# Weight rounding at the joints of side-by-side blocks, a gelu moved one block on, a root with more steps around it

## The chip, the cores and the metric

The kernel runs on one core of one Trainium2 chip. The metric is device time in microseconds (us) of one execution, the median of the runs shown. The engines are TensorE (PE, with its weight loads as PEld), VectorE (DVE), ScalarE (ACT), GpSimd (POOL), and SyncE (SP), which issues most DMAs. Each works through a queue of its own and waits for the others by semaphores.

## The reference, cut to what matters

Three transformer-like blocks on 512 tokens of 1024 channels. All of it is fp32. The change touches how the weights of six linears reach TensorE, and the two pieces of elementwise work below.

```python
# first block, mixer: retention, normed by head, gated, then the output linear
yr = _retention_chunkwise(qh, kh, v, log_gamma)
mu = jnp.mean(yr, axis=-1, keepdims=True)
var = jnp.mean(jnp.square(yr - mu), axis=-1, keepdims=True)
yr = (yr - mu) * lax.rsqrt(var + EPS)
y_ret = jax.nn.silu(g) * (yr * gn_w + gn_b)
y_mix = jnp.concatenate([y_ssd, y_ret], axis=-1) @ w_out
...
# third block, mixer: spatial gating, matrix memory and sparse attention, gated and summed
z = h @ w_in
def gmlp_mixer(u_pre, v_pre, ln_g, ln_b, ws, bs):
    u = jax.nn.gelu(u_pre)
    v = layer_norm(jax.nn.gelu(v_pre), ln_g, ln_b)
...
merged = sigmoid(ga) * y_a + sigmoid(gb) * y_b + sigmoid(gc) * y_c
```

## The kernel before

A linear reads its weights from HBM in slabs through a ring of two slots (`weight_ring`). Each tile of 128 output channels takes one unit of weights (128x1024; in `w3_up_a` 128x512). To keep fp32 precision with fast matmuls, ACT rounds a unit to its high half (`weights_hi`), POOL subtracts to get the low half (`weights_lo`), and PE makes three products of each of eight k steps: high by high, high by low activations, low by high. There are two buffers for units (UNITS = 2), so ACT rounds unit n+2 when PE is done with tile n. Activations are split in the same way, the high half on ACT (L780, L992) and the low half on DVE (L804, L1049).

`linears_beside` runs linears beside other work. It is called five times, one Block each, and every Block ends with a barrier of all engines:

| Block | linears, tiles | work beside | next linear |
|---|---|---|---|
| state space | w_z, 8 | state-space heads | w_g |
| retention | w_g, 8 | retention | w_mixu |
| mix | w_mixu, 8 | head norms of retention | w_mixr |
| sparse attention | mqk, mo, gu, gv, 24 | attention | w3_ga |
| gated memory | ga, gb, gc, 24 | spatial gating, matrix memory | w3_up_a |

The other work is written as generators, one for PE and one for ACT, which are cut into quanta by `yield`. A slot is one k step of three matmuls. `due` says how many quanta must have run by a slot: `min(quanta, 1 + int(slot * (quanta - 1) / (share * slots)))`. PE runs the quanta that are due behind a slot. ACT has no slots of its own: for tile n it runs all quanta that are due by the tile's last slot, then rounds unit n+2 (`high`, L770, which waits until PE is done with tile n), then takes the tile out of its bank (`take`, L1446 or the like). DVE runs its side work in one row.

`split_ahead` gives the rounding of the next linear's first units, `s.ahead` says to the next Block how many are there. Before the change it is called for both units, and ACT does this after everything else of the Block:

```python
            if beside.act_end:
                beside.act_end(act)
            act.wait_ge(s.units_done.sem, unit0 + count)
            next_high(act)
```

`act_end` is used once: sparse attention gives `gelu`, which applies gelu to `s.gv` (L3797).

In `mix` a head's mean and variance are matmuls (L1940, L1945), the squares are on ACT (L1974), the root is on ACT (L1977) and its reciprocal on DVE (L1997). `spreads` (L1952) puts it on all partitions, and DVE applies it (L2001, L2002). In gated memory the spatial gating is mean (L3134), centring (L3141), squares (L3146), variance (L3151), root (L3156), scaling (L3163), shift (L3169) and transposes (L3181). A head of the matrix memory is scores (L3261), weighing (L3300, L3303) and values (L3270), and `finish` (L3310 to L3312) frees the banks of the head before.

Of the kernel before, what the change touches and what calls it, by code (L numbers as in the profile page):

```python
# [18 lines left out]
ACT = mybir.ActivationFunctionType  # L19
# [3 lines left out]
P = 128  # L23
# [298 lines left out]
UNITS = 2  # L322
UNIT_K = 8
# [354 lines left out]
def linears_beside(s, parts, beside):  # L678

    ahead, s.ahead = s.ahead, 0
    tiles, fresh = [], None
# [23 lines left out]
    bank = lambda n: s.ps[n % 2]  # L708
    next_high, next_low = split_ahead(s)

# [8 lines left out]
    with s.nc.Block() as block:  # L719
# [38 lines left out]
        def _(act):  # L758
# [19 lines left out]
            if fresh:  # L778
                for k in range(fresh.tiles):
                    act.activation(fresh.hi(k), fresh.src(k), ACT.Copy).then_inc(s.act_hi.sem, 1)  # L780
            high(1)
            next(other)
            for n, (p, _, _, _) in enumerate(tiles):
                for k in range(p.kt):
                    slot += 1
                    while run < beside.due(slot, slots):
                        next(other)
                        run += 1
                if n + UNITS < count:
                    high(n + UNITS)  # L790
                take(n)
            for _ in other:
                pass
            if beside.act_end:
                beside.act_end(act)
            act.wait_ge(s.units_done.sem, unit0 + count)
            next_high(act)

# [609 lines left out]

def split_ahead(s):

    _, kt, width = PLAN[s.next_part]
    slab, units = s.first_slab[s.next_part], s.split_units
    w = s.ring[:, slab % RING, 0:kt * width].rearrange("p (k n) -> p k n", k=kt)
    tiles = [(u, k) for u in range(width // P) for k in range(0, kt, UNIT_K)][:UNITS]
    raw = [w[:, k:min(k + UNIT_K, kt), u * P:(u + 1) * P] for u, k in tiles]
    place = lambda x, n: x[(units + n) % UNITS][:, 0:min(kt, UNIT_K) * P].rearrange("p (k n) -> p k n", n=P)
    s.ahead = UNITS  # L1420

    def high(act):
        act.wait_ge(s.slab_ready[slab % RING], (slab // RING + 1) * 16)
        for n in range(UNITS):
            act.activation(place(s.w_hi, n), raw[n], ACT.Copy).then_inc(s.hi_made.sem, 1)

    def low(pool):
        for n in range(UNITS):
            pool.wait_ge(s.hi_made.sem, units + n + 1)
            pool.tensor_tensor(place(s.w_lo, n), raw[n], place(s.w_hi, n).bitcast(F32), ALU.subtract).then_inc(s.lo_made.sem, 1)  # L1430

    return high, low
# [495 lines left out]
def mix(s):  # L1928
# [25 lines left out]
    def on_pe(pe):  # L1954
        mean(pe, 0)
        mean(pe, 1)
        yield
        for h in range(heads):
            if h + 2 < heads:
                mean(pe, h + 2)  # L1960
            variance(pe, h)
            yield
        yield
        for h in range(heads):
            spreads(pe, h)
            yield

    def on_act(act):
# [8 lines left out]
        act.activation(std, s.ps[4][0:heads, :], ACT.Sqrt, bias=s.eps[0][0:heads, :], scale=1.0 / P).then_inc(std_ready.sem, 1)  # L1977
        yield
        for h in range(heads):
# [31 lines left out]
    def load_memory(sync):  # L2011
        sync.dma_start(flat(16), s.I["mem"]).then_inc(s.loaded.sem, 16)

    linears_beside(s, [part("w_mixu", Split(lambda k: s.u[:, k, :], 8, s.rounded(58), s.rounded(66)), store(lambda t: waiting[:, t, :]))],
                   Beside(18, 0.95, on_pe, on_act, on_dve, load_memory))
    for c, n in ((mean_ready, 8), (cen_ready, 8), (sq_ready, 8), (var_ready, 8), (std_ready, 2), (spread, 8), (applied, 8), (high_ready, 8)):
# [1102 lines left out]
class SpatialGating:  # L3119
# [11 lines left out]

    def mean(self, pe):
        for u in range(4):
            mm = pe.matmul(self.s.ps[6][:], self.s.ones, self.s.gv[:, u, :], start=u == 0, stop=u == 3)  # L3134
        mm.then_inc(self.mean_ready.sem, 1)
# [242 lines left out]
def gated_memory(s):  # L3378
# [10 lines left out]

    def on_pe(pe):  # L3390
        spatial.mean(pe)
        memory.turn_rows(pe)
# [29 lines left out]

    def on_act(act):
        for k in range(8):
            act.activation(s.conv_qk[:, k, :], s.conv_qk[:, k, :], ACT.Silu, bias=s.col("ml_conv_b")[:, k:k + 1]).then_inc(s.convolved.sem, 1)
# [40 lines left out]
    def on_dve(dve):  # L3466
# [5 lines left out]
        spatial.take(dve)  # L3472
        dve.wait_ge(s.opened.sem, s.opened.at(1))
        spatial.gate(dve, step)
# [7 lines left out]
        normed.turn_over(dve)  # L3482
        dve.wait_ge(s.opened.sem, s.opened.at(2))
        normed.finish(dve, step)

    def last_gate(act, step, t, ps):
        if t == 0:
# [4 lines left out]
    linears_beside(s, [part("w3_ga", h, store(lambda t: s.gate_a[:, t, :])), part("w3_gb", h, store(lambda t: s.gate_b[:, t, :])), part("w3_gc", h, last_gate)],  # L3492
                   Beside(22, 0.75, on_pe, on_act, on_dve, spatial.load))
    for x in (spatial, memory, normed):
        x.passed()
    s.convolved.passed(8)
    s.opened.passed(2)

# [213 lines left out]
def sparse_attention(s):  # L3712
# [12 lines left out]
    qk0 = s.tiles  # L3725
    gv_done = s.tiles + 20

# [66 lines left out]

    def gelu(act):
        act.wait_ge(s.evac_done.sem, gv_done)
        act.activation(s.gv, s.gv, ACT.Gelu_apprx_tanh)  # L3797

    def after_rows(dst):
# [11 lines left out]
        part("w3_gv", h, store(lambda t: s.gv[:, t, :])),  # L3811
    ], Beside(x.count + 4, 0.92, on_pe, on_act, on_dve, load_tables, gelu))
    x.passed()
# [80 lines left out]
```

## Time and profile before

| | us |
|---|---|
| median of 3 runs | 4124.14 |
| lowest and highest | 4122.24, 4129.01 |
| the profiled execution, its time | 4120.71 |
| its span | 4118.9 |

A row of the timeline gives the start and the length in us, the engine, the line, the operation, output and inputs, and in brackets how long the engine had been idle and what it waited for. Several instructions of one line in a row are merged, with x and their number. "PEq L719" is the barrier at the end of a `linears_beside` Block. In the views by stretch, PEclk is the granted clock of TensorE as a share of the full one: 1.00 is 2.4 GHz and 0.50 is 1.2 GHz.

### The profile page before, as it was taken

How to read it: one execution, taken by the hardware profiler on the slowest of the kernel's cores; microseconds unless marked ns; L12 is line 12 of the kernel's file. 1: busy time of each engine (PE TensorE's matmuls, PEld its weight loads, DVE VectorE, ACT ScalarE, POOL GpSimd, SP SyncE). 2: the span in 40 equal slices, each digit the busy share in tenths (PEclk: the TensorE clock that was granted, in tenths of full speed). 3: DMA queues.
4: the chain of work that ended last, by engine and by line, in shares of the span. 5: the costliest groups of instructions: out<-in, count | busy, mean ns of one | idle time of the engine just before them, and what ended most of it. 6: DMA issues, size and time to landing. Idle time of an engine off the chain costs nothing. (4 is left out here: it accounts for less than half of the span.)

```text
span 4118.9 us, 39706 instructions
## 1 busy us (share of the span) xinstructions
PE 3681.9 (89%) x14504; PEld 2462.0 (60%) x14504; DVE 2343.7 (57%) x4183; ACT 1485.5 (36%) x3057; POOL 1236.9 (30%) x844
## 2 busy tenths in 40 slices
PE   8888898999999999799777777777789998999999
PEld 6755586788788778443232232232257666677887
DVE  3673353677925373467777777777641763355361
ACT  1133244443232453144444444444431554333221
POOL 0012252344410014133333333333321222243443
PEclk9999999999989999899999999999999999999999
DMA  3211131224612222499999999999941211122222
GB/s 119 77 41 67 57 132 52 72 92 174 271 51 103 88 91 101 168 415 421 421 416 421 421 407 421 421 405 421 421 165 63 77 52 57 62 82 82 103 92 82
DMA packets 113966, 791.04 MB, mean 192 GB/s; under 512 B 13360, under 2 KB 13680, under 8 KB 22128
## 3 DMA queue, kind: packets, MB, share of 16 engines
q0 software_dynamic: 73728, 536.90, 31.5%
q1 hardware_dynamic: 40048, 251.63, 17.1%
q8 instruction: 116, 1.90, 0.2%
q14 instruction: 74, 0.61, 0.0%
HBM read 786.38 MB, written 2.10 MB: 191 GB/s over the span
## 5 line engine op out<-in xcount | busy, mean ns | idle before, releaser
L2852 PE MATMUL bank<-arena 128*128 128x512 f32 x1984 | 965.8, 614 | 264.7 <-ACT arena L2900 244.8
L965 PE MATMUL bank<-rounded,weights_hi 128*128 128x512 f32 (+1 forms) x2248 | 877.2, 390 | 43.1 <-DVE rounded L1049 16.0
L915 POOL TENSOR_TENSOR weights_lo<-weight_ring,weights_hi 128x1024 fp32r<-128x1024 f32 (+3 forms) x245 | 566.6, 2313 | 1109.0 <-ACT weights_hi L987 1108.8
L966 PE MATMUL bank<-rounded,weights_hi 128*128 128x512 f32 (+1 forms) x2248 | 868.3, 386 | 0.0
L967 PE MATMUL bank<-rounded,weights_lo 128*128 128x512 f32 (+1 forms) x2248 | 868.3, 386 | 0.0
L2852 PEld LDWEIGHTS bank<-arena 128*128 128x128 f32 x1984 | 348.3, 191 | 848.9 <-issue 828.3
L2944 DVE SCALAR_TENSOR_TENSOR arena<-arena,bank 128x1024 f32<-128x1024 f32 x512 | 624.6, 1221 | 341.2 <-DMA arena<-in_experts,arena 338.4
L2931 POOL DMA_INDIRECT arena<-in_experts,arena x512 | 480.7, 939 | 877.0 <-PE bank L2852 711.1
L987 ACT ACTIVATE weights_hi<-weight_ring 128x1024 fp32r<-128x1024 f32 (+3 forms) x297 | 299.1, 1007 | 947.8 <-PE bank L967 940.9
L965 PEld LDWEIGHTS bank<-rounded,weights_hi 128*128 128x128 f32 x2248 | 424.2, 189 | 147.9 <-issue 19.4
L967 PEld LDWEIGHTS bank<-rounded,weights_lo 128*128 128x128 f32 x2248 | 424.1, 189 | 85.9
L966 PEld LDWEIGHTS bank<-rounded,weights_hi 128*128 128x128 f32 x2248 | 424.5, 189 | 82.9 <-issue 0.5
L812 POOL TENSOR_TENSOR weights_lo<-weight_ring,weights_hi 128x1024 fp32r<-128x1024 f32 x62 | 149.4, 2410 | 704.1 <-ACT weights_hi L770 704.1
L2895 ACT ACTIVATE arena<-arena 128x1 f32<-128x1 f32 x512 | 104.0, 203 | 691.8 <-DVE arena L2944 691.5
L745 PE MATMUL bank<-rounded,weights_hi 128*128 128x512 f32 x544 | 231.2, 425 | 5.2 <-POOL weights_lo L812 5.2
L1049 DVE TENSOR_TENSOR rounded<-arena,rounded 128x512 fp32r<-128x512 f32 (+1 forms) x116 | 188.1, 1634 | 51.7 <-ACT rounded L992 51.5
L746 PE MATMUL bank<-rounded,weights_hi 128*128 128x512 f32 x544 | 216.6, 398 | 0.0
L747 PE MATMUL bank<-rounded,weights_lo 128*128 128x512 f32 x544 | 216.4, 398 | 0.0
L2900 ACT ACTIVATE arena<-base_tables,arena 128x128 f32<-128x128 f32 x496 | 199.6, 402 | 16.1
L2896 ACT ACTIVATE arena<-arena 128x1 f32<-128x1 f32 x512 | 151.3, 296 | 16.8
L1446 ACT ACTIVATE arena<-bank 128x512 f32<-128x512 f32 (+3 forms) x162 | 88.8, 550 | 189.9 <-PE bank L577 101.5
L745 PEld LDWEIGHTS bank<-rounded,weights_hi 128*128 128x128 f32 x544 | 104.8, 193 | 74.5 <-issue 52.1
(437 smaller groups left out, 4293.7 us busy)
## 6 DMA issues: line engine op xcount, KB each, us to landing
arena<-in_w_ada SPq DMA_DIRECT2D x48, 512.0 KB, 8.1
weight_ring<-in_w_up SPq DMA_DIRECT2D x22, 1024.0 KB, 5.0
weight_ring<-in_w_down SPq DMA_DIRECT2D x8, 1408.0 KB, 6.1
weight_ring<-in_w_ga SPq DMA_DIRECT2D x8, 1024.0 KB, 4.9
weight_ring<-in_w_gb SPq DMA_DIRECT2D x8, 1024.0 KB, 4.9
weight_ring<-in_w_q SPq DMA_DIRECT2D x8, 1024.0 KB, 9.1
arena<-in_experts,arena POOLq DMA_INDIRECT x512, 15.2
weight_ring<-in_w_mlp1a SPq DMA_DIRECT2D x8, 1024.0 KB, 4.8
```

The source lines that it names most:

```text
L745: pe.matmul(bank(n), hi[:, k, :], x.hi(k), start=first, stop=False)
L746: pe.matmul(bank(n), hi[:, k, :], x.lo(k), start=False, stop=False)
L747: mm = pe.matmul(bank(n), lo[:, k, :], x.hi(k), start=False, stop=last)
L915: eng.tensor_tensor(lo, raw(m), hi.bitcast(F32), ALU.subtract).then_inc(s.lo_made.sem, 1)
L965: pe.matmul(bank(n)[:, 0:p.n], hi[:, k - k0, :], x.hi(k), start=first, stop=False)
L966: pe.matmul(bank(n)[:, 0:p.n], hi[:, k - k0, :], x.lo(k), start=False, stop=False)
L967: mm = pe.matmul(bank(n)[:, 0:p.n], lo[:, k - k0, :], x.hi(k), start=False, stop=last)
L987: act.activation(hi, raw(m), ACT.Copy).then_inc(s.hi_made.sem, 1)
L2852: mm = pe.matmul(total[:, half * T:(half + 1) * T], diag[:, j, :], rows[:, j, D + half * T:D + (half + 1) * T], start=i % SLOTS == 0, stop ...
L2900: act.activation(diag[:, i % ROWS, :], s.eye, ACT.Copy, scale=weight[:, i:i + 1]).then_inc(s.diag_ready.sem, 1)
L2931: pool.indirect_dma_start(out=rows[:, j, :], out_offset=None, in_=s.I["experts"], in_offset=bass.IndirectOffsetOnAxis(ap=s.expert[:, i:i + ...
L2944: dve.scalar_tensor_tensor(row, row, 1.0, tokens(i // SLOTS), ALU.mult, ALU.mult, accum_out=dots[:, i:i + 1]).then_inc(s.dotted.sem, 1)
```

## The change

- `split_ahead` takes a count, and `linears_beside` asks for one unit. ACT rounds it as soon as PE is done with the last tile but one, ahead of that tile's `take`, and not behind the Block's other work. POOL's low half follows at once.
- The second unit is now rounded by the next Block as its unit 1: ahead of ACT's first quantum, or, where the input is rounded there too, behind the fifth of its tiles (in mix); in `linears_in_a_row` behind the input tiles.
- The gelu on `s.gv` becomes ACT's first quantum in gated memory. There PE's mean (L3134) moves to a second quantum and waits for it. All later quanta of both engines are one further on, of 23 in place of 22.
- In `mix` two yields are added on PE and ACT around the root, and the quanta become 20.

```diff
-    next_high, next_low = split_ahead(s)
+    next_high, next_low = split_ahead(s, 1)
...
                 for k in range(fresh.tiles):
                     act.activation(fresh.hi(k), fresh.src(k), ACT.Copy).then_inc(s.act_hi.sem, 1)
-            high(1)
+                    if k == 4:
+                        high(1)
+            else:
+                high(1)
...
                 if n + UNITS < count:
                     high(n + UNITS)
+                elif n + UNITS == count:
+                    act.wait_ge(s.units_done.sem, unit0 + n + 1)
+                    next_high(act)
                 take(n)
...
-            act.wait_ge(s.units_done.sem, unit0 + count)
-            next_high(act)
...
-def split_ahead(s):
+def split_ahead(s, count=UNITS):
...
-    s.ahead = UNITS
+    s.ahead = count
...
# mix, on_pe ahead of the spreads, and on_act behind the root
-        yield
+        for _ in range(3):
+            yield
...
-                   Beside(18, 0.95, on_pe, on_act, on_dve, load_memory))
+                   Beside(20, 0.95, on_pe, on_act, on_dve, load_memory))
...
# spatial gating
     def mean(self, pe):
+        pe.wait_ge(self.s.opened.sem, self.s.opened.at(1))
...
# gated memory
     def on_pe(pe):
+        yield
         spatial.mean(pe)
...
     def on_act(act):
+        act.activation(s.gv, s.gv, ACT.Gelu_apprx_tanh).then_inc(s.opened.sem, 1)
+        yield
...
-                   Beside(22, 0.75, on_pe, on_act, on_dve, spatial.load))
+                   Beside(23, 0.75, on_pe, on_act, on_dve, spatial.load))
...
# sparse attention
-    ], Beside(x.count + 4, 0.92, on_pe, on_act, on_dve, load_tables, gelu))
+    ], Beside(x.count + 4, 0.92, on_pe, on_act, on_dve, load_tables))
```

Lines of the changed kernel stand a few lines further down (L1425 is L1428 there, L770 L771, L780 L781, L1446 L1449, L1977 L1981, L3797 L3431).

ACT's queue from the end of the retention Block to the start of mix, before:

```order
L1817 ACTIVATE arena<-bank 128x2x512 [waits beside2]
L1446 ACTIVATE arena<-bank 128x512 [waits units_done]
L1425 ACTIVATE weights_hi<-weight_ring 128x1024 [waits slab_ready1,units_done]
L1425 ACTIVATE weights_hi<-weight_ring 128x1024
L719 UNCONDITIONAL_BRANCH
L757 UNCONDITIONAL_BRANCH [waits barrier_Pool_Activation_PE_DVE_SP_release]
L780 ACTIVATE rounded_152<-arena 128x512
L780 ACTIVATE rounded_158<-arena 128x512
L780 ACTIVATE rounded_164<-arena 128x512
L780 ACTIVATE rounded_170<-arena 128x512
L780 ACTIVATE rounded_176<-arena 128x512
L780 ACTIVATE rounded_182<-arena 128x512
```

and in the changed kernel (L1820 is the last L1817 of before, L1449 its L1446):

```order
L1428 ACTIVATE weights_hi<-weight_ring 128x1024 [waits slab_ready1,units_done]
L1449 ACTIVATE arena<-bank 128x512 [waits units_done]
L1820 ACTIVATE arena<-bank 128x2x512 [waits beside2]
L1449 ACTIVATE arena<-bank 128x512 [waits units_done]
L720 UNCONDITIONAL_BRANCH
L758 UNCONDITIONAL_BRANCH [waits barrier_Pool_Activation_PE_DVE_SP_release]
L781 ACTIVATE rounded_152<-arena 128x512
L781 ACTIVATE rounded_158<-arena 128x512
L781 ACTIVATE rounded_164<-arena 128x512
L781 ACTIVATE rounded_170<-arena 128x512
L781 ACTIVATE rounded_176<-arena 128x512
L771 ACTIVATE weights_hi<-weight_ring 128x1024 [waits units_done]
```

One rounding has moved ahead of the last two takes, the other behind the barrier and behind five of the eight input tiles.

ACT's queue in mix around the root, before (L1974 is a square, L1982 rounds a finished head):

```order
L1974 ACTIVATE arena<-arena 128x512 [waits beside3,beside1] x2
L770 ACTIVATE weights_hi<-weight_ring 128x1024 [waits units_done]
L1446 ACTIVATE arena<-bank 128x512 [waits units_done]
L1977 ACT_TABLE_LOAD
L1977 ACTIVATE arena<-bank,base_tables 8x512 [waits beside3]
L1982 ACTIVATE rounded_3277<-arena 128x512 [waits beside6]
L770 ACTIVATE weights_hi<-weight_ring 128x1024 [waits units_done,slab_ready0]
L1446 ACTIVATE arena<-bank 128x512 [waits units_done]
```

and in the changed kernel:

```order
L1978 ACTIVATE arena<-arena 128x512 [waits beside3,beside1]
L1981 ACT_TABLE_LOAD
L1981 ACTIVATE arena<-bank,base_tables 8x512 [waits beside3]
L771 ACTIVATE weights_hi<-weight_ring 128x1024 [waits units_done]
L1449 ACTIVATE arena<-bank 128x512 [waits units_done]
L771 ACTIVATE weights_hi<-weight_ring 128x1024 [waits units_done,slab_ready0]
L1449 ACTIVATE arena<-bank 128x512 [waits units_done]
L1987 ACTIVATE rounded_3282<-arena 128x512 [waits beside6]
```

The root stands ahead of a unit's rounding and a take that it stood behind, and two tiles lie between it and the first finished head.

ACT's queue from the end of sparse attention into gated memory, before:

```order
L3797 ACT_TABLE_LOAD
L3797 ACTIVATE arena<-arena 128x2048 [waits evac_done]
L1425 ACTIVATE weights_hi<-weight_ring 128x1024 [waits slab_ready0,units_done]
L1425 ACTIVATE weights_hi<-weight_ring 128x1024
L719 UNCONDITIONAL_BRANCH
L757 UNCONDITIONAL_BRANCH [waits barrier_Pool_Activation_PE_DVE_SP_release]
L3425 ACT_TABLE_LOAD
L3425 ACTIVATE arena<-arena,params_sb 128x512 x8
L3146 ACTIVATE arena<-arena 128x512 [waits spatial_centred] x4
L770 ACTIVATE weights_hi<-weight_ring 128x1024 [waits units_done,slab_ready1]
```

and in the changed kernel (L3431 is the gelu, L3434 the convolution's silu, L3152 the squares):

```order
L1428 ACTIVATE weights_hi<-weight_ring 128x1024 [waits slab_ready0,units_done]
L1449 ACTIVATE arena<-bank 128x512 [waits units_done] x2
L720 UNCONDITIONAL_BRANCH
L758 UNCONDITIONAL_BRANCH [waits barrier_Pool_Activation_PE_DVE_SP_release]
L771 ACTIVATE weights_hi<-weight_ring 128x1024 [waits units_done]
L3431 ACT_TABLE_LOAD
L3431 ACTIVATE arena<-arena 128x2048
L3434 ACT_TABLE_LOAD
L3434 ACTIVATE arena<-arena,params_sb 128x512 x8
L771 ACTIVATE weights_hi<-weight_ring 128x1024 [waits units_done,slab_ready1]
L1449 ACTIVATE arena<-bank 128x512 [waits units_done]
L3152 ACTIVATE arena<-arena 128x512 [waits spatial_centred] x4
```

The gelu has moved behind the barrier and behind the second unit's rounding, and the squares behind the first tile's take.

## Rows read from the trace of the kernel before

**Rows 1.** Waits of PE, 204 to 3640: us in total, times, longest.
```profile
PE bank L1940 <- PEq L719: 7.6, 1, 7.6
PE bank L1952 <- DVE arena L1997: 4.3, 1, 4.3
PE bank L3270 <- DVE arena L3312: 4.6, 3, 1.5
```

**Rows 2.** Timeline at the joint of state space and retention, DVE and PE.
```profile
313.48 0.75 DVE L1697 SCALAR_TENSOR_TENSOR arena<-arena,params_sb,bank 128x512 f32<-128x512 f32 x1 [1.90 <-PE bank L1690]
316.39 1.66 PE L1790 MATMUL bank<-arena 64*128 64x512 f32 x4 [2.95 <-PEq L719]
```

**Rows 3.** Timeline at the joint of retention and mix, ACT, POOL, DVE, PE.
```profile
402.24 0.59 ACT L1446 ACTIVATE arena<-bank 128x512 f32<-128x512 f32 x1
403.85 4.64 POOL L1430 TENSOR_TENSOR weights_lo<-weight_ring,weights_hi 128x1024 fp32r<-128x1024 f32 x2 [21.17 <-ACT weights_hi L1425]
408.82 4.28 ACT L780 ACTIVATE rounded<-arena 128x512 fp32r<-128x512 f32 x8 [4.10 <-PEq L719]
409.48 4.91 DVE L804 TENSOR_TENSOR rounded<-arena,rounded 128x512 fp32r<-128x512 f32 x8 [10.93 <-ACT rounded L780]
415.18 1.02 PE L1940 MATMUL bank<-arena,base_tables 128*128 128x512 f32 x2
```

**Rows 4.** Timeline in mix, a POOL subtraction and DVE beside it.
```profile
465.36 2.39 POOL L812 TENSOR_TENSOR weights_lo<-weight_ring,weights_hi 128x1024 fp32r<-128x1024 f32 x1 [11.84 <-ACT weights_hi L770]
466.00 2.30 DVE L2002 SCALAR_TENSOR_TENSOR arena<-arena,params_sb 128x512 f32<-128x512 f32 x1
```

**Rows 5.** Timeline in mix, the root's reciprocal on DVE.
```profile
453.58 3.34 DVE L1997 RECIPROCAL arena<-arena 8x512 f32<-8x512 f32 x1 [14.16 <-ACT arena L1977]
```

**Rows 6.** Timeline at the joint of mix and w_mixr, DVE and PE.
```profile
490.55 0.69 DVE L1989 TENSOR_TENSOR rounded<-arena,rounded 128x512 fp32r<-128x512 f32 x1 [0.67 <-ACT rounded L1985]
496.53 0.76 PE L965 MATMUL bank<-rounded,weights_hi 128*128 128x512 f32 x1 [7.16 <-PEq L719]
```

**Rows 7.** Timeline at the joint of sparse attention and gated memory, ACT and PE.
```profile
3400.19 0.60 ACT L1446 ACTIVATE arena<-bank 128x512 f32<-128x512 f32 x1 [4.84 <-PE bank L747]
3402.10 1.91 ACT L3797 ACTIVATE arena<-arena 128x2048 f32<-128x2048 f32 x1
3410.02 6.72 PE L3134 MATMUL bank<-arena,base_tables 128*128 128x512 f32 x8 [9.87 <-PEq L719]
3417.01 0.50 PE L745 MATMUL bank<-rounded,weights_hi 128*128 128x512 f32 x1
3426.67 3.59 PE L3151 MATMUL bank<-arena,base_tables 128*128 128x512 f32 x8
```

**Rows 8.** Timeline in gated memory, from tile 1's end to the transposes.
```profile
3431.67 1.06 ACT L770 ACTIVATE weights_hi<-weight_ring 128x1024 fp32r<-128x1024 f32 x1 [4.05 <-PE bank L747]
3441.30 2.72 ACT L3169 ACTIVATE arena<-arena,params_sb 128x512 f32<-128x512 f32 x4 [2.58 <-DVE arena L3163]
3444.40 1.91 PE L3181 MATMUL bank<-base_tables,arena 128*128 128x128 f32 x16
```

**Rows 9.** Timeline in gated memory, a head's scores and the wait for the finish.
```profile
3483.19 2.32 PE L3261 MATMUL bank<-arena 128*128 128x512 f32 x8
3492.26 0.69 DVE L3312 TENSOR_TENSOR arena<-bank,arena 128x512 f32<-128x512 f32 x1
```

**Rows 10.** Timeline at the joint of gated memory and w3_up_a, ACT.
```profile
3614.26 0.60 ACT L3489 ACTIVATE arena<-bank 128x512 f32<-128x512 f32 x1 [4.84 <-PE bank L747]
3618.27 2.19 ACT L992 ACTIVATE rounded<-arena 128x512 fp32r<-128x512 f32 x4 [2.37 <-PEq L719]
```

**Rows 11.** Stretches: us, busy PE, PEld, DVE, ACT, POOL (instructions), PEclk, DMA share, GB/s.
```profile
457.00:463.20 6.20, 6.20 (x12) 3.82 (x13) 1.50 (x2) 0.63 (x1) 0.00 (x0) 0.50 0.11 46
262.40:265.60 3.20, 3.20 (x15) 1.90 (x12) 2.15 (x4) 1.27 (x1) 0.00 (x0) 0.50 0.00 0
3493.10:3499.00 5.90, 5.90 (x20) 3.38 (x21) 0.26 (x1) 0.00 (x0) 0.00 (x0) 1.00 0.00 0
```

More of the change, by code:

```diff
@@ L1416, in split_ahead @@
     w = s.ring[:, slab % RING, 0:kt * width].rearrange("p (k n) -> p k n", k=kt)
-    tiles = [(u, k) for u in range(width // P) for k in range(0, kt, UNIT_K)][:UNITS]
+    tiles = [(u, k) for u in range(width // P) for k in range(0, kt, UNIT_K)][:count]
     raw = [w[:, k:min(k + UNIT_K, kt), u * P:(u + 1) * P] for u, k in tiles]
     place = lambda x, n: x[(units + n) % UNITS][:, 0:min(kt, UNIT_K) * P].rearrange("p (k n) -> p k n", n=P)
-    s.ahead = UNITS
+    s.ahead = count
     def high(act):
         act.wait_ge(s.slab_ready[slab % RING], (slab // RING + 1) * 16)
-        for n in range(UNITS):
+        for n in range(count):
             act.activation(place(s.w_hi, n), raw[n], ACT.Copy).then_inc(s.hi_made.sem, 1)
     def low(pool):
-        for n in range(UNITS):
+        for n in range(count):
             pool.wait_ge(s.hi_made.sem, units + n + 1)
@@ L1977, in on_act @@
         act.activation(std, s.ps[4][0:heads, :], ACT.Sqrt, bias=s.eps[0][0:heads, :], scale=1.0 / P).then_inc(std_ready.sem, 1)
-        yield
+        for _ in range(3):
+            yield
         for h in range(heads):
@@ L3423, in on_act @@
     def on_act(act):
+        act.activation(s.gv, s.gv, ACT.Gelu_apprx_tanh).then_inc(s.opened.sem, 1)
+        yield
         for k in range(8):
@@ L3472, in on_dve @@
         spatial.take(dve)
-        dve.wait_ge(s.opened.sem, s.opened.at(1))
+        dve.wait_ge(s.opened.sem, s.opened.at(2))
         spatial.gate(dve, step)
@@ L3482, in on_dve @@
         normed.turn_over(dve)
-        dve.wait_ge(s.opened.sem, s.opened.at(2))
+        dve.wait_ge(s.opened.sem, s.opened.at(3))
         normed.finish(dve, step)
@@ L3496, in gated_memory @@
     s.convolved.passed(8)
-    s.opened.passed(2)
+    s.opened.passed(3)
 class Compression:
@@ L3725, in sparse_attention @@
     qk0 = s.tiles
-    gv_done = s.tiles + 20
     def on_pe(pe):
@@ L3793, in load_tables @@
             sync.dma_start(dst, s.I[src]).then_inc(s.iota_loaded.sem, 16)
-    def gelu(act):
-        act.wait_ge(s.evac_done.sem, gv_done)
-        act.activation(s.gv, s.gv, ACT.Gelu_apprx_tanh)
     def after_rows(dst):
```

## The prediction

> **What bounds the kernel now.** I read the waits of PE first: the Blocks concerned lie in 204 to 3640, PE sits idle for little else there than the joints between Blocks and a few waits on DVE, and PE's queue sets the end of each Block. Then the timeline at each of the five joints, engine by engine, for what released the barrier. In all five it is POOL. At the joint of retention and mix ACT's last take ends at 402.83, POOL subtracts the two units from 403.85 to 408.49, and the next Block starts at 408.82, 0.33 later [rows 3]; PE had 7.6 us of idle [rows 1]. So a joint costs what the rounding takes behind the last work that remains. Last, the stretches, for the clock: the reader is to see that a PE wait is often followed by a stretch at 0.50 (1.2 GHz), where a matmul takes twice its time [rows 11].
>
> **The joints, one rounding out, one moved.** Ending a Block is now up to what is last without POOL. The first unit's rounding and subtraction start one tile earlier, and a tile is 8 slots of 0.69 us (the 14 slots from 3417.01 to 3426.67 [rows 7]), 5.5 us, against some 3.5 us for both. The slab it reads has been asked for two tiles before, so I add no wait.
> - State space to retention: DVE's L1697 is last and ends at 314.23; plus 0.35 the next Block starts at 314.6 and not 316.39 [rows 2]. Gain 1.8.
> - Retention to mix: ACT's take, 402.83, plus 0.33 is 403.2 and not 408.82 [rows 3]. Gain 5.6.
> - Mix to w_mixr: DVE's L1989 ends at 491.24, plus 0.35 is 491.6 and not 496.53 [rows 6]. Gain 4.9.
> - Sparse attention to gated memory: the take ends at 3400.79, start 3401.15 and not 3410.02 [rows 7]. Gain 8.9, the gelu's share included.
> - Gated memory to w3_up_a: the take ends at 3614.86, start 3615.19 and not 3618.27 [rows 10]. Gain 3.1.
>
> The second unit is rounded in the new Block, 1.06 us on ACT [rows 8] and 2.4 on POOL [rows 4]. PE wants it only behind the first tile, 5.5 us in (in w3_up_a a tile is half as long, but its inputs are rounded at DVE's pace of 0.61 a tile and hold it too). Cover is enough at all five, so nothing for PE. It delays ACT's first quantum by 1.0, and SP's load of the third slab until that subtraction is done; the load is wanted four tiles on, and costs nothing.
>
> **What the moved subtraction does to DVE.** In mix the second unit's rounding comes behind the fifth input tile: ACT is there 2.7 us into the Block (5 x 0.535), so POOL subtracts from 3.8 to 6.2. DVE's L804 for tiles 5 to 7 falls on it. DVE's L2002, with two SBUF inputs, took 2.30 us with POOL's L812 running from 465.36 to 467.75, and ended at 468.30, 0.55 behind POOL [rows 4]; an operation of that size beside no POOL work takes 0.75, as L1697 does [rows 2]. L804 has two SBUF inputs as well. So tile 5's low half ends near 6.75, tile 7's near 8.0, DVE's first centring at 8.6. PE's quantum behind slot 4 waits for that; before it started 6.36 into the Block (415.18 less 408.82 [rows 3]). Cost 2.3.
>
> The Trainium skill, GPSIMD Engine Reference, Specifications, says that GpSimd's SBUF interfaces are shared with VectorE, with contention for DVE instructions with two SBUF inputs. It speaks against this spot of the change, and the trace agrees (2.30 us in rows 4). Were there no contention, only the delay by ACT would be left, 0.6 us, and the sum 1.7 better.
>
> **The root in mix.** PE waits 4.3 us for the reciprocal [rows 1]. Quanta now come every 3.2 slots (60.8 / 19) and not every 3.58. The last variance moves from slot 29 to 26, the first spread from 36 to 39: 13 slots, 9 us. The chain in them is a table load of 1.3 (a take's end, 3400.79, to the gelu's start, 3402.10 [rows 7]), some 0.7 for the root, 3.34 for the reciprocal [rows 5], and up to 2 until the last variance has its square: 7.3. ACT also reaches the root within the tile of the last variance (order of ACT's queue), so the wait goes, with over 1.5 us to spare. What is late next is nothing: the last spread stays behind slot 61. With the wait goes its cold clock: 6.2 us at 0.50 [rows 11] did what 3.1 us do at full clock. Gain 4.3 + 3.1 = 7.4.
>
> **Gated memory.** PE used to start with the mean, 6.72 us for 8 matmuls at half clock; the same shape took 3.59 in the variance at full clock, and from the start to the first L745 6.99 [rows 7]. Now PE starts with tile 0, 1.0 us after the last matmul, so short a gap that I take the clock to hold (behind a wait of 1.54 us it stood at 1.00, third of rows 11). The mean comes behind slot 7, 4.9 us into the Block, at full clock: some 3.5 for the stage in place of 7.0. Gain 3.5. Its new wait is for the gelu: 1.06 for the second unit, 1.3 for the table, 1.91 [rows 7], done at 4.3. No wait, with 0.6 to spare; queued behind it would be the whole of PE.
>
> Behind it quanta come every 6.55 slots and not 6.86, and that takes cover from two places:
> - The transposes. ACT takes the root for the tile behind the variance's. Tile 1's end, 3431.67, to the last shift's end, 3444.02, is 12.35 us, and PE came at 3444.40 [rows 8]: 19 slots, from 16 to 35. Now the root starts behind slot 24 and the transposes are due behind slot 40: 16 slots, 10.9 us. New wait 1.5.
> - The heads. From a head's scores at 3483.19 to the end of L3312 at 3492.95 is 9.8 us [rows 9], and PE waited 1.5 three times with 7 slots between [rows 1]. New distances of the three heads that wait are 7, 6, 6 slots. 2 x 0.69 = 1.4 more.
> - The norm at the end keeps its slots (138 and 144).
>
> **The clock in new waits.** Three waits of 2.2 to 2.3 us now stand where there was a short one or none. A wait of 1.95 us was followed by over 3.2 us at 0.50, one of 1.54 by none [rows 11]. Bounds: nothing, or 3.1 us each as at the root. I take 1.6 (3.2 us at half) for two of three: 3.2. At the two joints that keep over 2 us of idle I take the clock to fall as before, no gain.
>
> **Sum.** 1.8 + 5.6 + 4.9 + 8.9 + 3.1 = 24.3 at the joints; less 2.3; plus 7.4; plus 3.5; less 1.5 + 1.4; less 3.2: gain 26.8 us. The profiled execution took 4120.71, the changed one would take 4093.9. The median of the runs stands 3.4 above the profiled one, so 4097.3.
>
> **Rivals.**
> - The clock holds. For: two of the joints fall from over 5 us of idle to 2.2 and 2.5. Then nothing is lost in the new waits (+3.2), and the two joints give back the half-clock stretch behind them (2.3 and 1.9). Gain 34: 4090.
> - The cover is thinner than I count. For: the gelu has only 0.6 us, and ACT runs long rows of work ahead of its units in gated memory. If mean, units or shifts come 2 us late and the clock falls after each, at some four places, 12 us go. Gain 15: 4109.
> - The change doesn't do what it says: the next slab isn't in the ring, or ACT is late for the last tile but one, so that the rounding ends as late as before. Against: SP's load for it stands two tiles ahead. Then only root and mean are left, less the new waits: gain 5, 4119.
> - Slower: the half clock stays in the head stretch. Waits of 2.2 us come back every 20 us there, from 3464 to 3547. If the clock were at 0.50 throughout, 83 us of PE work would take up to 83 more, and the result would be near 4180. It decides from about 30 us of lost time, which is 60 us at half. Against: it stayed at 1.00 behind 1.54 us [rows 11], and the falls that I read end within 3 to 6 us.
>
> **How the numbers follow.** Forecast 0.62, clock holds 0.14, thin cover 0.17, not as it says 0.03, slower 0.02, and 0.02 for the rest. The range goes from 4087 (clock holds, less 3 for the runs' scatter) to 4109 (thin cover); the bounds of the clock (0 to 9.3) and of DVE's delay (0.6 to 2.3) lie within. A measurement tells about 0.2%, 8 us, from no change: faster takes the first three cases, 0.93; same takes 0.05; slower 0.02.
>
> **What would show it.** In the profile after: no PE wait over 3 us at L719; POOL's next-unit subtraction beside the last tile; DVE's L804 near 2.5 us long for one tile, and PE waiting about 2 us at the third mean in mix; no wait at the first spread; the mean at about 3.6 us for 8; waits of 1.5 at the transposes and 2.2 at two L3270. Wrong would be a wait of PE on the gelu, or half clock for over 15 us in gated memory.

## The result, and the profile after

| us | before | after |
|---|---|---|
| median | 4123.39 (4 runs) | 4092.22 (4 runs) |
| lowest and highest | 4122.24, 4129.01 | 4090.39, 4096.64 |
| the profiled execution, its time | 4120.71 | 4093.84 |
| its span | 4118.9 | 4092.1 |

Of the executions of the root's change alone, further down, one in ten took 7352.1 us; it isn't counted in the median there.

The ratio of the times is 0.9924, with a 95% interval from 0.9908 to 0.9940: 31 us faster, and the interval reaches from 25 to 38. 4097.3 was forecast, in a range from 4087 to 4109. From one profiled execution to the other the gain is 26.8 us, the figure of the prediction's sum. Its term for the clock was wrong in every place, though, and two losses were left out; a gain at the joint of mix and w_mixr, which it had put at nothing, made up for them. So the stretches have to be looked at one by one.

First PE's waits after, 204 to 3620, us in total, times, longest. They answer to [rows 1]; L3276, L1943, L720 are L3270, L1940, L719 of before.

```profile
...
PE bank L3276 <- DVE arena L3318: 6.0, 3, 2.2
...
PE bank L1943 <- DVE arena L2000: 3.8, 1, 3.8
...
PE bank L970 <- PEq L720: 2.2, 1, 2.2
...
PE bank L1943 <- PEq L720: 1.9, 1, 1.9
PE bank L1793 <- DVE arena L1802: 1.8, 1, 1.8
...
PE bank L3370 <- DVE arena L3364: 1.6, 1, 1.6
...
PE bank L3187 <- ACT arena L3175: 1.5, 1, 1.5
...
PE bank L1793 <- PEq L720: 1.1, 1, 1.1
PE bank L746 <- PEq L720: 1.1, 1, 1.1
```

The barriers, which had held PE for 3.0, 7.6, 7.2 and 9.9 us, hold it for 1.1, 1.9, 2.2 and 1.1. The wait at the root of mix is no longer in the list. New are the 3.8 us at L1943, the third mean, the 1.8 us at L1793 in retention, and the 1.5 us at L3187, the transposes, which were forecast.

The joint of retention and mix after, ACT, POOL, DVE and PE, which answers to [rows 3]:

```profile
401.74 0.59 ACT L1449 ACTIVATE arena<-bank 128x512 f32<-128x512 f32 x1
...
402.64 1.96 PE L1943 MATMUL bank<-arena,base_tables 128*128 128x512 f32 x4 [1.86 <-PEq L720]
...
403.28 3.10 DVE L809 TENSOR_TENSOR rounded<-arena,rounded 128x512 fp32r<-128x512 f32 x5 [5.23 <-ACT rounded L781]
...
405.24 1.05 ACT L771 ACTIVATE weights_hi<-weight_ring 128x1024 fp32r<-128x1024 f32 x1
406.36 2.37 POOL L817 TENSOR_TENSOR weights_lo<-weight_ring,weights_hi 128x1024 fp32r<-128x1024 f32 x1 [12.41 <-ACT weights_hi L771]
406.84 3.64 DVE L809 TENSOR_TENSOR rounded<-arena,rounded 128x512 fp32r<-128x512 f32 x3 [0.46 <-ACT rounded L781]
...
410.41 1.28 DVE L2000 SCALAR_TENSOR_TENSOR arena<-bank,arena 128x512 f32<-128x512 f32 x2
411.14 2.08 PE L1943 MATMUL bank<-arena,base_tables 128*128 128x512 f32 x2 [3.80 <-DVE arena L2000]
```

The take ends at 402.33 and PE starts at 402.64; no rounding stands between. DVE needs 3.10 us for five tiles (0.62 each) and 3.64 for the three beside POOL's subtraction. The third mean starts 8.50 us into the Block.

The joint of sparse attention and gated memory after, which answers to [rows 7]:

```profile
3379.72 2.39 POOL L1433 TENSOR_TENSOR weights_lo<-weight_ring,weights_hi 128x1024 fp32r<-128x1024 f32 x1 [5.91 <-ACT weights_hi L1428]
...
3384.01 0.60 ACT L1449 ACTIVATE arena<-bank 128x512 f32<-128x512 f32 x1 [3.89 <-PE bank L748]
...
3384.89 1.06 ACT L771 ACTIVATE weights_hi<-weight_ring 128x1024 fp32r<-128x1024 f32 x1 [0.28 <-PEq L720]
3385.97 1.28 ACT L3431 ACT_TABLE_LOAD   x1
3387.27 1.92 ACT L3431 ACTIVATE arena<-arena 128x2048 f32<-128x2048 f32 x1
...
3389.92 3.59 PE L3140 MATMUL bank<-arena,base_tables 128*128 128x512 f32 x8
```

POOL's subtraction for the next linear ends at 3382.11, 2.5 us before the last take does. The gelu ends at 3389.19, 0.7 us before the mean that needs it, and the mean runs without a wait and at full clock, 3.59 for 6.72.

Now where the 26.8 us came from, by PE's gaps and starts in the two traces:

| stretch | gain, us |
|---|---|
| PE's gap at five joints: 2.95, 7.56, 7.16, 9.87, 5.54 before, 1.10, 1.86, 2.18, 1.09, 2.42 after | 24.4 |
| up to the end of state space | -1.0 |
| retention, 84.89 to 85.21 | -0.3 |
| mix, 80.53 to 77.99 | 2.5 |
| behind the joint of mix and w_mixr, 49.97 to 47.81 | 2.2 |
| gated memory, 204.21 to 205.98 | -1.8 |
| the rest | 0.8 |

Stretches for the clock, after, with the columns of [rows 11] (PEclk is the third figure from the end):

```profile
410.00:416.00 6.00, 4.86 (x7) 1.47 (x8) 2.38 (x4) 1.23 (x2) 0.00 (x0) 0.50 0.38 158
457.00:463.20 6.20, 6.20 (x22) 3.52 (x20) 3.67 (x5) 1.65 (x4) 2.00 (x1) 1.00 0.01 3
482.80:487.00 4.20, 4.19 (x18) 3.46 (x19) 0.00 (x0) 1.05 (x1) 2.40 (x1) 1.00 0.00 2
3489.20:3495.00 5.80, 5.78 (x19) 3.33 (x20) 0.14 (x1) 0.00 (x0) 0.00 (x0) 1.00 0.00 0
3549.50:3560.40 10.90, 10.86 (x18) 5.63 (x19) 6.71 (x8) 3.06 (x3) 2.72 (x1) 0.53 0.26 98
```

Before, 457.0 to 463.2 was the stretch at half clock behind the root's wait [rows 11]; now the same times begin 3.6 us behind the start of the first spread, which had no wait, and PE runs 22 matmuls at full clock in place of 12. Behind the joint of mix and w_mixr, at 482.8, and behind a 2.2 us wait at 3489.2 the clock held. It was at half behind the third mean's wait, and for 10.2 us of the 10.9 behind the last spread of gated memory (L3370, which puts the root of the memory's norm on all partitions). In what follows, "the clock fell" means that it went from full to half.

### The profile page after: what moved, and what is told of

Same layout as the page of the kernel before. It is cut to its first block and busy times, and to the rows that moved or that the text cites. A ratio compares the mean times of both kernels' runs of the same rounds, so it can differ in the third digit from the quotient of the medians.

```text
span 4092.1 us, 39706 instructions
## 1 busy us (share of the span) xinstructions
PE 3675.7 (90%) x14504; PEld 2459.4 (60%) x14504; DVE 2342.3 (57%) x4183; ACT 1486.2 (36%) x3057; POOL 1240.9 (30%) x844
## 5 line engine op out<-in xcount | busy, mean ns | idle before, releaser
L1449 ACT ACTIVATE arena<-bank 128x512 f32<-128x512 f32 (+3 forms) x162 | 88.7, 550 | 177.0 <-PE bank L577 101.8
```

## The experiments

A ratio is to the kernel before, run beside it on the same chip; there the kernel before took 4121.9, 4121.6 and 4121.8 us (median). The executions of one kernel scatter by 3 to 8 us, once by 12, and their half-clock stretches differ from one to the next, so a difference of 3 us between two medians says little, and where it matters the traces are read.

### The three parts of the change, each alone

The joints alone: the kernel before, with one unit rounded ahead, beside the last tile, and the other one in the next Block.

```diff
-    next_high, next_low = split_ahead(s)
+    next_high, next_low = split_ahead(s, 1)
...
-            high(1)
+                    if k == 4:
+                        high(1)
+            else:
+                high(1)
...
+                elif n + UNITS == count:
+                    act.wait_ge(s.units_done.sem, unit0 + n + 1)
+                    next_high(act)
...
-            act.wait_ge(s.units_done.sem, unit0 + count)
-            next_high(act)
```

> The kernel before with the one-unit rounding alone (gelu at the Block's end, old quanta). Theory: joints shrink by 1.8, 5.7, 5.0, 5.7 and 3.1 us, 21.3 together; in mix 2.2 us and a fall of the clock are lost to POOL and DVE; the wait for the root (4.3) stays and so does the half clock behind it; w_mixr behind the joint runs at full clock (2.2 more). Total gain 19 to 22. Rival (each joint's idle only moves to the next wait): gain under 10.

Measured: 4100.39 us (4099.05 to 4103.15), ratio 0.9949, interval [0.9932, 0.9966]; 21.5 us less than before. PE's waits, 204 to 3620:

```profile
...
PE bank L1954 <- DVE arena L1999: 4.3, 1, 4.3
PE bank L3136 <- PEq L719: 4.2, 1, 4.2
...
PE bank L1942 <- DVE arena L1997: 3.8, 1, 3.8
```

The root's wait of 4.3 is still there, the third mean's 3.8 is there already, and the joint of sparse attention keeps 4.2 us, in which ACT loads the table and does the gelu. So the third mean's new wait belongs to the moved rounding, and to nothing else in the change.

The root alone: the kernel before, with the two yields added and 20 quanta in mix.

```diff
-        yield
+        for _ in range(3):
+            yield
...
-                   Beside(18, 0.95, on_pe, on_act, on_dve, load_memory))
+                   Beside(20, 0.95, on_pe, on_act, on_dve, load_memory))
```

> The kernel before with the two added yields around the root in mix alone (20 quanta). Theory: the wait of 4.3 us at the first spread goes, and the 6.2 us at half clock behind it run in 3.1: mix 7.4 us shorter, the total too. Rival (the wait comes back at a later spread or at the joint): under 3 us.

Measured: 4115.04 us (4112.06 to 4117.99), ratio 0.9986, [0.9976, 0.9995]; 6.5 us less. In its trace mix goes from 80.53 to 73.19 us, 7.3 less, where the prediction had 7.4. PE's waits in mix, 406 to 480, are the whole list:

```profile
PE bank L1940 <- PEq L719: 7.6, 1, 7.6
PE bank L1945 <- ACT arena L1975: 0.8, 1, 0.8
```

Nothing came in the root's place.

The gelu alone: the kernel before, with the gelu as ACT's first quantum in gated memory, PE's mean in a second one, and 23 quanta.

```diff
     def on_pe(pe):
+        yield
         spatial.mean(pe)
...
     def on_act(act):
+        act.activation(s.gv, s.gv, ACT.Gelu_apprx_tanh).then_inc(s.opened.sem, 1)
+        yield
...
-                   Beside(22, 0.75, on_pe, on_act, on_dve, spatial.load))
+                   Beside(23, 0.75, on_pe, on_act, on_dve, spatial.load))
```

> The kernel before with the gelu moved into gated memory alone (23 quanta, mean behind slot 7). Both units are still rounded at the end. Theory: the joint's idle falls from 9.9 to 6.7 us; tile 0 starts at half clock in place of the mean, so less than 3.5 is won there (the mean at 3.6, but some 3 us lost on tile 0); new waits of 1.5 at the transposes and 0.7 each at two values: total gain 0 to 2 us. Rival: the mean waits for the gelu; then a wait at the mean of over 1 us and no gain.

Measured: 4124.61 us (4121.26 to 4129.14), ratio 1.0009, [1.0000, 1.0019]: no gain, if anything 3 us more. PE's first tile and its mean behind the joint:

```profile
3406.61 0.76 PE L745 MATMUL bank<-rounded,weights_hi 128*128 128x512 f32 x1 [6.80 <-PEq L719]
...
3414.11 3.60 PE L3135 MATMUL bank<-arena,base_tables 128*128 128x512 f32 x8
```

and PE's waits, 3390 to 3600:

```profile
...
PE bank L3271 <- DVE arena L3313: 6.0, 3, 2.2
PE bank L3365 <- DVE arena L3359: 1.6, 1, 1.6
PE bank L3182 <- ACT arena L3170: 1.5, 1, 1.5
```

The joint is 3.1 us shorter (6.8 for 9.9) and the mean takes 3.60. But PE still idles for 6.8 us, the two roundings, so the half clock is there all the same; it now lies on the first tile, 5 us at 0.50:

```profile
3406.60:3411.60 5.00, 4.99 (x12) 3.93 (x13) 0.00 (x0) 4.96 (x5) 0.00 (x0) 0.50 0.76 275
```

That is 2.5 us given back of the 3.1 at the mean. The new waits, 1.5 at the transposes and 1.4 more at the values, take about as much again. Behind one of the 2.2 us waits the clock fell (0.66 over 5 us, 1.7 us of work), and behind the last spread it stayed at half for 10.2 us in place of 6.8 (another 1.7).

**The mean at full clock needs both the moved gelu and the short joint.** With the joints alone the mean stands right behind 4.15 us of idle and is slow; with the gelu alone the first tile is. This is the mean with the joints alone:

```profile
3394.14 6.33 PE L3136 MATMUL bank<-arena,base_tables 128*128 128x512 f32 x8 [4.15 <-PEq L719]
```

The joint and gated memory together take 214.1 us before, 208.0 with the joints alone, 217.1 with the gelu alone and 207.1 with both. So on top of the shorter joints the moved gelu was worth 1.0 us in these traces: its new waits, and the longer half clock at the last spread, took most of what it gave. By medians the parts alone give 21.5 + 6.5 - 3.0 = 25.0 and the whole 29 to 31. The difference has the sign of the first tile's 2.5 and of the one fall's 1.7, but with this scatter the medians don't show that it is they.

The changed kernel, measured again beside the last two:

> The changed kernel as it is, for a comparison in one call with e6_both. About 0.9925 of before.

Measured: 4092.61 us (4089.84 to 4101.97), ratio 0.9930, [0.9916, 0.9943]. Its profiled execution is the slowest of the five. The waits and the clock behind each are those of the first trace: 3.77 and half clock at the third mean, 2.18 and full clock behind the joint of mix, 2.21 and 2.22 and full clock at the values, 1.62 and a long half clock at the last spread. Of the 8.1 us by which its span exceeds the first one's, 7.0 lie between the joints of mix and of gated memory, with some 20 us more at half clock there.

### Who holds DVE at the start of mix

The second unit's rounding behind the eighth input tile and not the fifth:

```diff
-                    if k == 4:
+                    if k == fresh.tiles - 1:
```

> The changed kernel with the second unit's rounding in mix behind all eight input tiles and not behind the fifth. Theory (POOL's subtraction holds DVE's two-input operations): POOL starts at about 5.3 us into the Block, DVE's last low half has begun by then, the three last low halves take 1.9 us together and not 3.6, the third mean in mix starts about 6.4 us into the Block (8.5 in the changed kernel), PE waits 1.6 and not 3.8 there, and the fall of the clock behind the wait goes or shrinks: mix is 2 to 5 us shorter. Rival (ACT's one instruction more is what delays DVE): the last three low halves come as late as the rounding made them, so the third mean stays within 0.5 us of 8.5.

Measured: 4090.87 us (4088.79 to 4094.16), ratio 0.9927, [0.9910, 0.9943]. DVE and PE behind the joint, which is at 401.95:

```profile
402.58 4.90 DVE L809 TENSOR_TENSOR rounded<-arena,rounded 128x512 fp32r<-128x512 f32 x8 [5.23 <-ACT rounded L781]
407.22 2.48 POOL L817 TENSOR_TENSOR weights_lo<-weight_ring,weights_hi 128x1024 fp32r<-128x1024 f32 x1 [13.97 <-ACT weights_hi L771]
407.41 1.28 DVE L2000 SCALAR_TENSOR_TENSOR arena<-bank,arena 128x512 f32<-128x512 f32 x2
408.14 1.12 PE L1943 MATMUL bank<-arena,base_tables 128*128 128x512 f32 x2 [1.49 <-DVE arena L2000]
```

All eight take 4.90, as before the change, and PE's wait is 1.49 for 3.80. The clock stays at 1.00:

```profile
402.00:410.00 8.00, 6.51 (x20) 3.24 (x20) 6.79 (x11) 6.37 (x11) 2.48 (x1) 1.00 0.38 132
```

Mix takes 73.06 us and not 77.99: 2.3 of waiting and 2.6 of half clock. L2000 reads the bank and one tile in SBUF, starts 0.19 behind POOL's subtraction and takes its 0.64 a tile as ever.

The whole is only 1 to 2 us faster than the changed kernel, within the scatter: behind the joint of mix and w_mixr the clock now fell, and the stretch there that took 47.81 us takes 49.40.

This alone doesn't separate POOL from ACT, since both have moved. So the rounding went back behind the fifth tile, and only POOL waits, until DVE has all eight:

```diff
+                if fresh and n == 1:
+                    pool.wait_ge(s.act_lo.sem, s.act_lo.at(fresh.tiles))
```

> The changed kernel, in mix POOL waits for DVE's eight low halves before it subtracts the second unit; ACT's order is untouched. Theory (POOL holds DVE): the low halves run on at 0.6 us each behind ACT's gap, third mean at about 6.9 us into the Block. Rival (ACT's order is the cause): nothing changes, third mean at 8.5.

Measured: 4084.59 us in its one execution, so that only its trace counts here. The Block starts at 398.69:

```profile
401.29 1.05 ACT L771 ACTIVATE weights_hi<-weight_ring 128x1024 fp32r<-128x1024 f32 x1
402.88 1.89 DVE L809 TENSOR_TENSOR rounded<-arena,rounded 128x512 fp32r<-128x512 f32 x3 [0.45 <-ACT rounded L781]
404.93 2.35 POOL L819 TENSOR_TENSOR weights_lo<-weight_ring,weights_hi 128x1024 fp32r<-128x1024 f32 x1 [14.93 <-DVE rounded L809]
405.44 1.13 PE L1945 MATMUL bank<-arena,base_tables 128*128 128x512 f32 x2 [2.03 <-DVE arena L2002]
```

The same three tiles take DVE 1.89 us and not 3.64. That is the cause shown: POOL's subtraction held DVE for 1.75 us, and ACT's rounding between the tiles accounts for the 0.45 of idle and no more. In the changed kernel's trace all of it lies in the first of the three, taken by itself here:

```profile
406.84 2.44 DVE L809 TENSOR_TENSOR rounded<-arena,rounded 128x512 fp32r<-128x512 f32 x1 [0.46 <-ACT rounded L781]
```

It ends at 409.28, 0.55 behind POOL (408.73), as L2002 did in [rows 4]. The other two take 0.68 each, as every tile does without POOL.

The Trainium skill, GPSIMD Engine Reference, Specifications, says that VectorE and GpSimd share SBUF interfaces, to the cost of DVE instructions with two SBUF inputs; by the 1.89 against 3.64 the traces agree. L2000, which has one input in a bank, ran beside POOL at its usual 0.64.

### The waits in gated memory and the clock behind them

The share of gated memory at 0.77 and not 0.75, so that the quanta stand nearly as far apart as before the change (6.7 slots; 6.9 before, 6.55 in the changed kernel):

```diff
-                   Beside(23, 0.75, on_pe, on_act, on_dve, spatial.load))
+                   Beside(23, 0.77, on_pe, on_act, on_dve, spatial.load))
```

> The changed kernel with the share of gated memory at 0.77 and not 0.75, so that quanta come every 6.72 slots. Theory (the waits there are a matter of slots between quanta): the wait at the transposes falls from 1.5 to 0.8 us (17 slots), the three at the values are 1.5 each and not 1.5, 2.2, 2.2 (7 slots each), the wait at the last spread (1.6) goes since it now lies 12 slots behind the tile whose end starts the root and not 8, and with it the half-clock stretch behind it (PEclk 0.61 over 13 us in the changed kernel). Gated memory 3.7 us shorter from the waits, up to 5 more from the clock. Rival: the waits are set by something else (POOL, the units) and stay; then no change.

Measured: 4094.44 us (4089.67 to 4097.45), ratio 0.9936, [0.9920, 0.9953]; its profiled execution is its fastest, with a span of 4087.9. PE's waits, 3390 to 3600:

```profile
PE bank L3276 <- DVE arena L3318: 4.6, 3, 1.5
...
PE bank L3337 <- DVE arena L3318: 2.2, 1, 2.2
PE bank L3187 <- ACT arena L3175: 0.8, 1, 0.8
```

The values wait 1.5 three times as before the change, the transposes 0.8, and the last spread no longer. But a wait of 2.2 stands at L3337, the means of the memory's norm, which need the last head's finish, and the clock falls behind it (0.66 over 5 us from 3523.9). Gated memory takes 203.23 us for 205.98 in the changed kernel. The medians don't show this gain of 2.7: this one is 2 us above the changed kernel's. Of the waits, the three at the values and the one at the last spread came as expected; the one at L3337 hadn't been foreseen.

Both edits together, the rounding behind the eighth tile and the share of 0.77:

> The changed kernel with both edits: the second unit in mix behind all eight input tiles, and share 0.77 in gated memory. If the two add up as the theory has it: 2 to 5 us in mix, 4 to 9 in gated memory, so 6 to 14 us less than the changed kernel. If a fall of the clock only moves to another wait: under 4.

Measured: 4087.64 us (4085.82 to 4089.14), ratio 0.9919, [0.9906, 0.9933]; 5.0 less than the changed kernel beside it, where 6 to 14 had been expected. Mix takes 73.06 us, gated memory 203.17. The 2.18 at L3337 is there again, with half clock behind, and behind the joint of mix the clock fell as well.

POOL's wait and the share of 0.77:

> The changed kernel with two edits: in mix POOL waits, before it subtracts the second unit, until DVE has rounded all eight low halves of the input; and the share of gated memory is 0.77. It asks whether the single 4084.6 of the POOL wait holds in more runs. DVE is held by POOL in mix: the third mean comes 6.7 us into the Block with a wait of about 2.0 and the clock at 1.00 behind it, mix takes some 73 us, and the whole 5 us less than the changed kernel, 4087 to 4088. A rival: the 4084.6 was more than scatter, POOL's wait is worth more than moving the rounding behind the eighth tile, and the whole is 4083.

Measured: 4087.08 us (4083.92 to 4089.49), ratio 0.9917, [0.9903, 0.9930]. The 4084.6 of POOL's wait was one run in a scatter of this width; moving the rounding and holding POOL back are worth the same. Here, behind a 2.04 us wait at the third mean, the clock fell for some 3.4 us, where it had held behind 2.03 with POOL's wait alone.

The rounding behind the eighth tile and the share at 0.80, where all quanta stand 7 slots apart:

> The changed kernel with two edits: the second unit rounded behind the eighth input tile in mix, and the share of gated memory at 0.80, where all its quanta stand 7 slots apart. At 0.77 a wait of 2.17 us stood at the norm's means (121 slots against 108 for the last values, now 126 against 112), with half clock behind it. If each wait follows from the slots alone, one slot more takes 0.69 of it: 1.5 us are left there, the three waits at the values stay at 1.5, none at the transposes and the last spread, and the clock behind 1.5 us holds: gated memory some 2.5 us shorter than at 0.77, the whole 4085. The rival: the half clock comes at some wait anyway, and nothing changes within 1 us, 4087.5.

Measured: 4087.82 us (4083.78 to 4091.29), ratio 0.9915, [0.9902, 0.9929]. PE's waits, 3380 to 3600:

```profile
PE bank L3276 <- DVE arena L3318: 5.0, 3, 1.9
...
PE bank L3370 <- DVE arena L3364: 0.2, 1, 0.2
```

The wait at L3337 is gone, where 1.5 had been expected to be left, and gated memory takes 202.15 us, 1.0 less than at 0.77. The expected 2.5 and the 4085 didn't come: one of the waits at the values is 1.9, not 1.5, and the clock fell behind that one instead. ACT's exps for that head (L3282) now come right behind a unit's rounding and a take; that this makes the wait longer is likely and not shown. The best versions are level at 4087 to 4088, some 4 to 5 us below the changed kernel and 34 below the one before.

Over the eleven traces other than the first one of the kernel before, this is how often the clock fell behind a wait (a stretch of 1 us under 0.90 among the four that follow PE's restart):

| wait of PE | us | fell |
|---|---|---|
| values; transposes; third mean | 1.5 | never |
| retention's decay table | 0.9 to 2.9 | never |
| joint of retention and mix | 1.9 | never |
| last spread, gated memory | 1.6 | 7 of 7 |
| state space (L1693) | 1.95 | 11 of 11 |
| third mean, POOL held back | 2.03, 2.04 | 1 of 2 |
| joint of mix and w_mixr | 2.2 | 4 of 9 |
| values | 1.9 | 1 of 1 |
| values | 2.2 | 1 of 10 |
| norm's means | 2.2 | 3 of 3 |
| joint of gated memory | 2.4 | 8 of 9 |
| third mean | 3.8 | 4 of 4 |

The length of a wait of 1.6 to 2.9 us doesn't tell whether the clock falls; the place does better. The four falls behind the joint of mix are those of the four kernels in which the clock hadn't fallen within mix, and it held in all five in which it had. Why isn't shown.

## Why the prediction came out

**Right, and by its own steps, save for the clock.** The joints: PE's gaps shrank by 1.85, 5.70, 4.98, 8.78 and 3.12, where 1.8, 5.6, 4.9, 8.9 and 3.1 were worked out from the last work that remains and the 0.33 to 0.35 behind it. The root: mix alone 7.3 shorter for 7.4. The gelu: 0.7 to spare for 0.6, the mean 3.59. The waits counted in slots: 1.48 at the transposes for 1.5, 2.21 and 2.22 at two of the values for 2.2. DVE's hold in mix: one L809 of 2.44 for "near 2.5", the third mean 8.50 into the Block for 8.6. One reading at the prediction's start holds for these Blocks alone: in 204 to 3640 PE also waits 245 us for ACT (L2852, from 1730 to 3032), between them and as long after the change.

**The clock's term failed in each of its places.** It had 3.2 for two of three waits of 2.2 to 2.3. Behind the two at the values the clock held, in the same kernel twice and in two variants more. The third, the third mean's, measured 3.8: the prediction took the place at which PE used to come, 6.36 into the Block, but that had been at half clock. Behind a joint of 1.86 PE ran at full clock and came at 4.7, so the wait was longer, though the loss by it no larger. That wait brought a full fall, 2.6 us. And the price for the fall was set at 1.6. The rows that the term went by were too few: the trace of the kernel before also has a wait of 1.62 us, at the last spread of gated memory, with 6.8 us of half clock behind it, between the 1.54 and the 1.95 that it cited and longer than the "3 to 6 us" in which it took the falls to end.

**Two losses were left out.** In retention ACT, PE and DVE start earlier, but the decay table doesn't come earlier. SP issues its load at 315.52, behind the barrier, 0.8 us sooner than before, and DVE starts on it 4.62 us later, for 3.58 before. PE waits for DVE.

```profile
320.14 1.29 DVE L1802 TENSOR_TENSOR arena<-bank,arena 128x512 f32<-128x512 f32 x2 [4.88 <-DMA arena<-in_decay]
321.48 0.92 PE L1793 MATMUL bank<-arena 64*128 64x384 f32 x4 [1.79 <-DVE arena L1802]
```

So the full clock behind this joint, which the prediction didn't count, bought nothing here. In the nine traces with the short joint this wait was 0.9 to 2.9 us long, and retention took 84.3 to 86.2 us, the more the longer the wait.

And the half clock behind the last spread, which was there before the change too, lasted some 3.5 us longer, 10.2 for 6.8 us; over 10.9 us that is a mean of 0.53 for 0.69, or 1.7 us. In the eight traces with this wait the fall lasted the longer the sooner it set in: 10.2 us where it began 0.4 to 0.6 us behind PE's restart (the changed kernel twice, the rounding behind eight, the gelu alone), 6.8 at 1.7 to 2.2 (before, joints alone, root alone), 3.4 at 3.7 (POOL's wait). In the trace of POOL's wait gated memory took 202.64 us, 3.3 less than in the changed kernel, with the same waits. What sets the moment isn't settled.

```profile
3574.40:3585.30 10.90, 10.88 (x26) 6.37 (x27) 6.91 (x8) 3.05 (x3) 2.35 (x1) 0.69 0.28 98
```

(That is the kernel before; the same length after stands in the stretches above.)

**A gain left out made up for them.** "At the two joints that keep over 2 us of idle I take the clock to fall as before": at mix and w_mixr it held, 2.2 us; at w3_up_a it fell. This half of the rival "the clock holds" came true, and it isn't something one could count on, since in four of nine traces it fell there.

With the sizes measured the sum reads: joints 24.4; mix 2.5 (the root's 7.3, less 2.2 for the later third mean and 2.6 for the clock behind it); the clock behind mix 2.2; gated memory -1.8 (the mean's 3.5, less 2.9 of waits, less 1.7 behind the last spread, and 0.7 that I can't assign); all else -0.5. That is 26.8. The agreement is earned in the terms of work and waits, and chance in those of the clock: 3.2 was counted as lost, 2.6 and 1.7 were lost in other places and 2.2 was won. It is chance too that this execution was the profiled one: the changed kernel's other profiled execution took 4101.97 us, with the same waits at the places of the change. The median lies 5 us below 4097.3: 3.4 had been added because the runs of before stood above their profiled one, while those of the changed kernel stand 1.6 below it.

## What to carry to other kernels

At a barrier, work out what ends last once the preparation for the next block is gone; the gains so worked out held at five joints to 0.15 us. Before moving a POOL elementwise operation into a block, see which two-input DVE operations lie under it and who waits for them: here a later place, or POOL held back, gave back 2.8 to 4.9 us of mix, by whether the clock held there. A step moved out of a gap gains only if the gap that remains is short enough for the clock; alone, the gelu's move gained nothing, and on top of the shorter joints 1.0 us.

## What the runs showed of the hardware

The half clock is not a matter of the wait before it alone: behind 1.6 us at the last spread it came each time, behind 1.95 us in state space too, and behind 2.2 us at the values in one of ten. By the count above it begins up to 4 us behind PE's restart, and it lasted from 3.4 us to 10.2. At the third mean's 3.8 us it set in while PE was still idle in three of four traces; in the changed kernel PE then ran its first 5.6 us at half.

A POOL subtraction of 128x1024 holds a DVE operation with two SBUF inputs until some 0.55 us behind its own end (1.89 us for three tiles free of it, 3.64 beside it), while one with an input in a bank wasn't held (two tiles of L2000 in 1.28 us beside it).

A table load on ACT before the gelu took 1.28 us, and the gelu started 0.02 behind it.
